# A decoder step on one core: convolution projected by block with its products on VectorE, embedding projections moved ahead of their gate

## The reference, cut to what matters

```python
xn = rmsnorm(h, g_mix)
z = xn @ w_in
q, k, v, og, lr, cv = jnp.split(z, SPLITS, axis=-1)
...                                   # gated linear attention gives o
a, gate = jnp.split(cv, 2, axis=-1)
u = a * jax.nn.sigmoid(gate)
c, buf_new = causal_depthwise_conv(u, buf0, w_conv, b_conv)   # 31 taps, 512 channels
c = jax.nn.silu(layernorm(c, g_conv_ln, b_conv_ln))
h = h + jnp.concatenate([o, c], axis=-1) @ w_out
xn = rmsnorm(h, g_ffn)
h = h + hier_moe(xn, ...)             # 32 experts, 2 for each row
xn = rmsnorm(h, g_ple)
h = h + jax.nn.sigmoid(xn @ w_ple_gate) * (p_l @ w_ple_proj)
...
return rmsnorm(h, g_final)
```

## Time and profile before

| | before |
|---|---|
| median of 3 runs | 1126.66 us (1126.3 to 1128.25) |
| the profiled execution's own time | 1125.14 us |
| its span in the trace | 1123.3 us |
| busy share of the span | TensorE 90%, VectorE 64%, ScalarE 42%, GpSimd 26% |

### The profile page before, as it was taken

How to read it: one execution, slowest core, us unless ns; L and a number is a source line. 1 busy time by engine, 2 the same in 40 slices (tenths; PEclk the granted TensorE clock), 3 DMA queues, 4 the chain that set the end, 5 groups by cost and what they waited for, 6 DMA issues and landing times.

```text
span 1123.3 us, 14888 instructions
## 1 busy us (share of the span) xinstructions
PE 1008.9 (90%) x4992; PEld 546.8 (49%) x4992; DVE 721.1 (64%) x830; ACT 473.6 (42%) x721; POOL 295.3 (26%) x267
## 2 busy tenths in 40 slices
PE   4899979999999978999429999999999999399996
PEld 3555535555555545555314555544444454144442
DVE  6259866667667596443586777776667675556552
ACT  7333122323222542322315655566555454434553
POOL 0567234656511522111011222222222223000000
PEclk9999989999999969999659999999999999699998
DMA  7443040000000602222647999999999977523321
GB/s 256 123 133 124 3 19 1 1 0 0 0 0 1 213 36 75 75 83 90 268 179 277 391 380 366 342 368 361 361 365 361 355 290 259 222 89 102 108 69 60
DMA packets 52234, 191.13 MB, mean 170 GB/s; under 512 B 19601, under 2 KB 20898, under 8 KB 37218
## 3 DMA queue, kind: packets, MB, share of 16 engines
q1 hardware_dynamic: 41250, 172.76, 43.6%
q0 software_dynamic: 10944, 17.85, 4.4%
HBM read 181.50 MB, written 31.09 MB: 189 GB/s over the span
## 4 chain that ended last, share of the span: by engine, by line
PE 63%; DVE 15%; DMA 11%; issue 4%; ACT 4%; POOL 2%; DVEq 1%; SPq 0%; POOLq 0%; ACTq 0%
PE psum L1691 12%; PE psum L1920 11%; PE psum L1999 8%; PE psum L1834 8%; DVE arena L1238 6%; DMA arena<-xn,ids 6%; PE psum L1938 6%; PE psum L1907 3%; PE psum L1989 2%; PE psum L1876 1%; PE psum L1758 1%; PE psum L1757 1%; DVE arena L1511 1%; DMA arena<-in_w_ple 1%; PE psum L1761 1%
## 5 line engine op out<-in xcount | busy, mean ns | idle before, releaser
L1920 PE MATMUL psum<-arena 128*128 128x512 f16 x888 | 201.8, 385 | 4.4 <-DVE arena L1515 4.4
L1238 DVE SCALAR_TENSOR_TENSOR arena<-arena,wc x120 | 185.9, 1549 | 17.3 <-DVE arena L1238 17.0
L1511 DVE TENSOR_TENSOR arena<-arena 128x1024 f16<-128x1024 f32 x148 | 174.2, 1217 | 2.6 <-ACT arena L1077 2.6
L1691 PE MATMUL psum<-arena 128*128 128x512 f16 (+1 forms) x864 | 153.1, 331 | 0.6 <-ACT arena L914 0.6
L1077 ACT ACTIVATE arena<-arena 128x1024 f16<-128x1024 f32 x148 | 147.1, 1047 | 0.0
L1920 PEld LDWEIGHTS psum<-arena 128*128 128x128 f16 x888 | 87.6, 99 | 104.6 <-DVE arena L1515 5.0
L1938 PE MATMUL psum<-arena 128*128 128x512 f32 x296 | 133.2, 593 | 1.2 <-DVE arena L1549 1.2
L1691 PEld LDWEIGHTS psum<-arena 128*128 (+1 forms) x864 | 68.2, 98 | 78.2 <-issue 8.7
L1683 PE MATMUL psum<-arena 128*128 128x384 f16 x576 | 96.3, 331 | 4.4 <-DVE arena L1205 2.4
L1999 PE MATMUL psum<-arena 128*128 128x512 f16 x432 | 96.8, 385 | 2.5 <-DVE arena L1620 2.5
L800 POOL DMA_INDIRECT yrows<-arena,idy x31 | 35.0, 1130 | 239.6 <-DVE arena L1549 232.0
(11 more groups left out here) (239 smaller groups left out, 1267.2 us busy)
## 6 DMA issues: line engine op xcount, KB each, us to landing
arena<-in_w_gu SPq DMA_DIRECT2D x74, 1024.0 KB, 9.3
arena<-in_w_dn SPq DMA_DIRECT2D x37, 1024.0 KB, 7.2
arena<-yrows SPq DMA_DIRECT2D x18, 512.0 KB, 4.7
side<-in_w_tok SPq DMA_DIRECT2D x16, 388.0 KB, 3.3
arena<-in_x SPq DMA_DIRECT2D x9, 512.0 KB, 4.4
side<-in_x SPq DMA_DIRECT2D x9, 512.0 KB, 4.0
xn<-arena SPq DMA_DIRECT2D x9, 512.0 KB, 2.9
out_y<-arena SPq DMA_DIRECT2D x9, 512.0 KB, 3.0
```

The lines of the kernel that those rows point to most:

```text
L1238: dve.scalar_tensor_tensor(acc, src, w[:, k:k + 1], acc, ALU.mult, ALU.add).then_inc(conv, 1)
L1511: dve.tensor_tensor(wsp[s][1][:, part], wgu[s][:, part], wsp[s][0][:, part], ALU.subtract).then_inc(ws_lo, 1)
L1691: x = pe.matmul(out, xnT[w][:, k, bass.ds(n * P, P)], wtok[m][:, k, col:col + width], start=k + w + m == 0, stop=k == KC - 1 and w == 1)
L1920: x = pe.matmul(psum[:, 2 + s, :], xgT[s][w][:, k, :], wsp[s][m][:, k, :], start=k + w + m == 0, stop=k == KC - 1 and w == 1)
```

## The change

In the conv stage TensorE's groups are taken by block: gate and a of one block of 384 rows, then the next block, in banks 2b and 2b+1. The first block is put between the transposes of tiles 3 to 8. ScalarE evacuates only the gate (the sigmoid); VectorE multiplies a straight from PSUM by it (`glu_rows`), and VectorE takes over both low parts of the splits. GpSimd keeps only the split of the first chunk, both halves of it. 18 taps of each of chunks 0 and 1 stand in this stage (`REST` is 13 instead of 9), four between one block and the next, so 88 taps (11 a step) are left for the attention stage. The transfers of the first chunk's weights and of the identity matrix come earlier.

For the embedding, `w_proj` and all nine tiles of `pT` are loaded in the router stage into buffers that the attention left. All nine projections run on TensorE between the experts and the gate; ScalarE copies each from PSUM to SBUF (`proj_out`), in turns with the split of `w_ple`, and `finish` reads that copy.

```diff
+        prj = [at(w, D) for w in [R4, R4 + D, RT + 2048, *[R1 + D * k for k in range(2, 6)], R4 + 7992, R4 + 7992 + D]]
...
+        wproj = [[th[:], qk[:]], [PT[:].rearrange("p a b -> p (a b)"), v_sb[0][:]]]
...
+            for k in range(PC):
+                for half in range(2):
+                    sp.dma_start(wproj[k][half], a["w_proj"][:, k, half * 512:(half + 1) * 512]).then_inc(pT_in, 16)
+            for n in range(NT):
+                sp.dma_start(pT[n], a["pT"][n]).then_inc(pT_in, 16)
             load_gu(2, 0, 2)
...
             def load_ple():
-                sp.dma_start(wproj, a["w_proj"]).then_inc(pw_in, 16)
...
+            pl.wait_ge(wcv_in, 16)
+            pl.tensor_copy(wcv[0][0], wcv_raw).then_inc(wcv_hi, 1)
+            pl.wait_ge(wcv_hi, 1)
+            pl.tensor_tensor(wcv[0][1], wcv_raw, wcv[0][0], ALU.subtract).then_inc(wcv_lo, 1)
...
+                for b in range(NBLK):
+                    if c >= 1:
+                        act.wait_ge(u_rdy, 4 * (c - 1) + GLU[b])
+                    act.wait_ge(cv_ps, 6 * c + 2 * b + 1)
+                    act.activation(sg_sb[:, b * BLK:(b + 1) * BLK], psum[:, 2 * b, 0:BLK], ACT.Sigmoid).then_inc(cv_sb, 1)
+                    for k, half in pieces_beside(c, b):
+                        split_wt(k, half)
...
+            def proj_out(n):
+                act.wait_ge(pr_ps, n + 1)
+                if n >= 3:
+                    act.wait_ge(wl_lo, KC + n)
+                act.activation(prj[n].rearrange("p (a b) -> p a b", b=512), psum[:, 4 - 2 * (n % 2):6 - 2 * (n % 2), :],
+                               ACT.Copy).then_inc(pr_sb, 1)
...
-            REST = 9
+            REST = 13
...
+            def block_done(c, b):
+
+                if b == 0 and c + 1 < CC:
+                    split_cv(c + 1)
+                glu_rows(c, b)
+                for k, half in pieces_beside(c, b):
+                    split_wt(k, half)
+
+            for b in range(NBLK):
+                block_done(0, b)
+            STEP = 4
+            for i in range(2 * (K - REST)):
+                taps(i // (K - REST), i % (K - REST), 1, i)
+                if i % STEP == STEP - 1:
+                    n = NBLK + i // STEP
+                    block_done(n // NBLK, n % NBLK)
...
-                dve.tensor_tensor(mixd[j], mixd[j], psum[:, 4:6, :].rearrange("p a b -> p (a b)"), ALU.mult).then_inc(mix_rdy, 1)
+                dve.wait_ge(pr_sb, n + 1)
+                dve.tensor_tensor(mixd[j], mixd[j], prj[n], ALU.mult).then_inc(mix_rdy, 1)
...
             def embed(n, j):
                 gate_half(n, j, 0)
-                if late(n, 1):
-                    project_p(n, j)
                 if not (isinstance(n, int) and n == NT - 1):
                     turn_x3(n + 1, 1 - j)
                 gate_half(n, j, 1)
...
+            pe.wait_ge(u_rdy, 4 * CC)
             pe.wait_ge(wt_lo, 2 * KC)
...
+            pe.wait_ge(pT_in, 16 * (2 * PC + NT))
+            for n in range(NT):
+                project_p(n)
+                if n == 6:
+                    turn_x3(0, 0)
             pe.wait_ge(wl_lo, 2 * KC)
+            pe.wait_ge(pr_sb, NT - 1)
             embeds(pe, embed)
```

More of the change, by code:

```diff
@@ L302, in bass_decoder_step @@
         og = [at(RT + 2304, VW), v_sb[1][:]]
+        wproj = [[th[:], qk[:]], [PT[:].rearrange("p a b -> p (a b)"), v_sb[0][:]]]
+        pT = [*[side[1][:, PC * j:PC * (j + 1), :] for j in range(KC // PC)],
+              *[v_sb[1][:, PLE * j:PLE * (j + 1)].rearrange("p (a b) -> p a b", b=P) for j in range(VW // PLE)],
+              *[x[:].rearrange("p (a b) -> p a b", b=P) for x in (E2, la, absx)]]
         wr = sb("wr", KC, G + NE)
@@ L444, in bass_decoder_step @@
         pw_in = sem("pw_in")
-        pT_in = [sem(f"pT_in{j}") for j in range(2)]
+        pT_in = sem("pT_in")
+        pr_sb = sem("pr_sb")
         add_rdy = sem("add_rdy")
-        std3_rdy = sem("std3_rdy")
-        rst3_rdy = sem("rst3_rdy")
         xn3_rdy = sem("xn3_rdy")
@@ L470, in rows, with pieces_beside @@
             return t[bass.ds(n * P, P), :]
[L472 to L483, removed]
+        def pieces_beside(c, b):
+            k = NBLK * c + b
+            return [(k, half) for half in range(2)] if k < KC else []
         block = ctx.enter_context(nc.Block())
@@ L511, in _ @@
             sp.dma_start(brb[:], a["b_router"].to_broadcast([P, G + NE])).then_inc(c_in, 16)
+            for k in range(1, KC):
+                if k % NBLK == 0:
+                    load_cv(k // NBLK + 1)
+                for half in range(2):
+                    load_wt(k, half)
             for cc in range(CC):
                 sp.dma_start(us[:, cc, :, 0:HIST], a["state_conv"][:, cc]).then_inc(hist_in, 16)
[L514 to L518, removed]
             sp.wait_ge(zero, 1)
@@ L684, in _ @@
             pl.memset(St[:], 0.0).then_inc(zero, 1)
[L685 to L706, removed]
+            pl.wait_ge(wcv_in, 16)
+            pl.tensor_copy(wcv[0][0], wcv_raw).then_inc(wcv_hi, 1)
+            pl.wait_ge(wcv_hi, 1)
+            pl.tensor_tensor(wcv[0][1], wcv_raw, wcv[0][0], ALU.subtract).then_inc(wcv_lo, 1)
+            pl.wait_ge(wcv_lo, 1)
+            pl.wait_ge(u_rdy, 4 * CC)
             pl.memset(oraw[NS:P, NT - 1, :], 0.0).then_inc(zero, 1)
@@ L907, in _ @@
                     split_cv(c + 1)
[L908 to L913, removed]
-                        act.activation(dst[:, b * BLK:(b + 1) * BLK], psum[:, 3 * part + b, 0:BLK], fn).then_inc(cv_sb, 1)
+                for b in range(NBLK):
[5 more added lines that the diff above has]
+                        split_wt(k, half)
             def lr_out(n):
@@ L1177, in _, with split_gate @@
             act.wait_ge(wple_in, 16 * KC)
-            for k in range(KC):
+            def split_gate(k):
                 if k == 1:
@@ L1190, in _ @@
         def _(dve):
-            dve.wait_ge(g1_in, 32)
+            dve.wait_ge(g1_in, 16)
             def norm_x(n, j):
@@ L1669, in transpose_x, with conv_part @@
                 x.then_inc(xT_ps, 1)
-            tiles(pe, transpose_x)
+            def conv_part(c, b, part, chunks):
+                col = P - P * part
+                for k in chunks:
+                    for w, m in PASSES:
+                        x = pe.matmul(psum[:, 2 * b + part, 0:BLK], wcv[c % 2][w][:, k, col:col + P],
+                                      xnT[m][:, k, b * BLK:(b + 1) * BLK], start=k + w + m == 0,
+                                      stop=k == KC - 1 and w == 1)
+                return x
@@ new lines, in _ @@
+            for n in range(4):
+                transpose_x(n, n % 2)
+            pe.wait_ge(wcv_lo, 1)
+            pe.wait_ge(xnT_v, 3)
+            for part in range(2):
+                for q in range(2):
+                    x = conv_part(0, 0, part, range(4 * q, 4 * q + 4))
+                    if q:
+                        x.then_inc(cv_ps, 1)
+                    n = 4 + 2 * part + q
+                    transpose_x(n, n % 2)
+            pe.wait_ge(xnT_v, 6)
+            for part in range(2):
+                for q in range(2):
+                    x = conv_part(0, 1, part, range(4 * q, 4 * q + 4))
+                    if q:
+                        x.then_inc(cv_ps, 1)
+                    elif part == 0:
+                        transpose_x(NT - 1, 0)
```

125 lines of the change are left out of this document (72 added, 53 removed).

## The result

The changed kernel took 1107.03 us (median of 4 runs, 1106.55 to 1108.17), the kernel before on the same chip 1126.49 us. The ratio is 0.9825, with a 95% interval of 0.9808 to 0.9842: faster by 19.5 us, where 13 were forecast. The span of the profiled execution fell from 1123.3 to 1104.9 us, so 18.4 us are to be accounted for.

What follows compares the result with a forecast made beforehand. Bounds: VectorE's late, slow list ending the conv stage, and a VectorE-ScalarE circle in the embedding. Terms -12.8 + 0.7 + 0 - 1.0 = -13.1 take 1125.14 to 1112.0; plus 1.5 to the median, about 1113.5 us, range 1105 to 1122.

Steps and rivals of the forecast that it cites:

- term 1: Conv stage into the attention: the first `turn` comes 12.8 us earlier, between 9 and 17.
- 36 taps at 1.28 + 0.18: Conv stage, VectorE's list: taps of 1.28 us with gaps of 0.18 take 52.7 us.
- TensorE waits some 7 us for VectorE: End of the conv stage: TensorE's blocks end near 123, VectorE's last product at 130.2.
- the 1.7 us for waking: Start of the attention: TensorE, waking from idle, loses 1.4 to 2 us before the first `turn`.
- term 2: Attention stage: eleven taps a step instead of ten are covered by reserves, costing 0.7 us in all.
- term 3: Router stage: 1.9 MB more loads cost 0 us, or 5 us without the DMA engines' idle time as cover.
- term 4: Embedding, with projections moved ahead of the gate: 1.0 us less, between 3 less and 2 more.
- the circle: Embedding loop: VectorE and ScalarE hand each tile to and fro, 14.45 to 14.8 us a tile.
- (a): Embedding loop: TensorE alone bounds it, -22.5 us in place of -1.0, about 1092 us; 6%.
- (b): Conv stage: slow taps or late transfers put the last product at 140; gain only 3, about 1123 us; 7%.
- (c): Embedding loop: TensorE's clock falls; mildly, 2 us a tile, mostly hidden; throughout, about 1183 us; 4%.
- (d): Router stage's loads not covered, or experts' gathers fall worse: 5 us more, 1118.5 us; 10%.

Runs made afterwards that it cites:

- experiment 5: The changed kernel with the 16 low parts of the attention weights back on GpSimd; 1102.89 us, ratio 0.9785.
- experiment 7: The changed kernel with 28 taps in the conv stage instead of 36 and 12 in each attention step; 1110.7 us, ratio 0.9863.
- experiment 6: The changed kernel with all transposes first and then the conv blocks in order; 1114.71 us, ratio 0.9892.
- experiment 3: The kernel before with the conv stage's taps written out instead of a hardware loop; 1120.47 us, ratio 0.9954.
- experiment 8: The changed kernel with the gate's sigmoid ahead of a later tile's square and the root's table loaded right after it; 1093.08 us, ratio 0.9697.
- Experiment 4: The changed kernel with the embedding gate's sigmoid replaced by a plain copy, so without its table loads; 1087.71 us, ratio 0.9652.

## Why the prediction was right, and where its terms were off

**The bound at the end of the conv stage (term 1)** was predicted at -12.8 us and measured at -19.6. The mechanism held: TensorE's wait for VectorE's taps went, block 0 moved between the transposes, GpSimd's absence made taps short. The step that failed is "36 taps at 1.28 + 0.18", and with it "TensorE waits some 7 us for VectorE". The 0.18 belongs to the hardware loop, and the changed list is written out: seven groups of four took 5.24 each, and the two with a chunk's shorter first tap 4.8 and 4.6, 46.1 in place of 52.7. The first tap came 2.2 us later than forecast (59.89), the last product 5.0 earlier (125.18 against 130.2), and by then VectorE was waiting for TensorE. Experiments 5 and 7 show it from both sides: slower taps or fewer of them leave the first `turn` at 144.1 to 144.2, and experiment 6 shows that what delays TensorE's list moves it one for one. Since TensorE hardly idles, the 1.7 us for waking did not fall due either. The two make 4.7 at the start of the projections (125.60 against 130.3) and 2.1 behind it. I had the count of instructions between two taps in front of me, in the listing of VectorE's order, and priced the new list by the old one's gap.

The cast on GpSimd, taken at 4 us between bounds of 2 and 4.06, took 2.73, and the subtraction 4.06 again. The rest of it went elsewhere, in the timeline of the change:

```profile
12.02 2.73 POOL L683 CAST arena<-arena 128x2048 f16<-128x2048 f32 x1 [9.97 <-DMA arena<-in_w_cv]
...
14.84 4.06 POOL L685 TENSOR_TENSOR arena<-arena 128x2048 f16<-128x2048 f32 x1
...
15.17 4.82 DVE L1199 SCALAR_TENSOR_TENSOR arena<-arena,rst,g 128x1024 f32<-128x1024 f32 x1 [0.15 <-DVE rst L1195]
...
24.00 4.00 PE L1713 MATMUL psum<-arena 128*128 128x384 f16 x12 [0.79 <-DVE arena L1205]
```

VectorE's scaling of a tile stood beside the subtraction and took 4.82 us where others took 1.28. Block 0 started at 24.00, not 21.

**Eleven taps a step (term 2)**: +0.7 predicted, +1.5 measured at the last `scores`. The steps themselves took it without a wait, as forecast; the last tap was mis-sized. I had set VectorE's slack of 0.81 us against it. But it stands ahead of qkT too, where no slack was left: TensorE's wait there grew from 2.23 to 3.71, by one whole tap. Another 1.5 us between the first and the last `turn` are the fourth long step (1.58 us), and 2.2 more came by the first `gate_up`. There too a lower clock is part of it: eight transposes at 425.70 took 1.97 us after the change and 1.09 at the same place before. The prediction had no term for this. The experts then gave 1.1 us back. That is within what this stage varies by with the same instructions: from the first `gate_up` to the first projection it took 367.3 us in experiment 3, 372.1 before, 371.0 after and 373.8 in experiment 8.

**Router stage (term 3)**: 0 predicted and measured. From the last of the router's matmuls to the experts' first transposes it is 34.67 us against 34.54. The DMA engines did the added 1.9 MB and stood still before `load_gu(2)` was issued at 562.78, as said. The columns are those of the earlier trace rows:

```profile
552.00:558.00 6.00, 0.54 (x9) 0.41 (x9) 5.69 (x13) 0.00 (x0) 0.00 (x0) 0.50 0.74 243
558.00:564.00 6.00, 0.54 (x9) 0.41 (x9) 5.26 (x12) 0.00 (x0) 2.57 (x2) 0.50 0.13 14
```

**Embedding (term 4)**: -1.0 predicted, -3.0 measured, within its bounds. The timeline of the change:

```profile
941.78 1.02 PE L2050 MATMUL psum<-th,side 128*128 128x512 f32 x2
...
973.55 5.34 PE L2060 MATMUL psum<-arena 128*128 128x512 f16 x24
...
980.87 1.22 DVE L1657 TENSOR_TENSOR arena<-psum,arena 128x1024 f16<-128x1024 f32 x1 [6.05 <-ACT arena L1129]
...
1010.91 5.35 PE L2060 MATMUL psum<-arena 128*128 128x512 f16 x24 [2.51 <-DVE arena L1657]
...
1025.57 7.04 PE L2060 MATMUL psum<-arena 128*128 128x512 f16 x24 [2.67 <-DVE arena L1657]
...
1093.99 1.02 ACT L1135 ACTIVATE arena<-psum 128x1024 f32<-128x1024 f32 x1 [3.42 <-PE psum L2060]
```

The nine projections ran through, and the gate started 31.8 us behind the first of them (32.4 forecast). Tile 1's `x3T_out` came 5.1 us later against the first projection than before (5.8). Then seven tiles to 1082.15 took 101.3 us, 14.47 each, where I had written 102.6 for "14.45 to 14.8" (1.3 of the difference), and from there it was 11.84 to the sigmoid (11.8). Experiment 4 shows that the circle set this.

**The rivals.** (a) fell: it needs the circle out of the way, and with its table loads gone the kernel took 1087.7 us, TensorE alone setting the time of the first tiles only. (b) fell, the last product being at 125.18. (c) held in its mild form: at two tiles (1025.57 and 1069.04) the granted clock fell after a wait and 24 matmuls took 7.04 us instead of 5.35. Both were covered by the circle and cost nothing at the end. The Trainium skill, TensorE: Matmul & The Clock Gate, "HAM oscillation — how this bites in real kernels", describes a fall at every step of a loop that waits some 3 to 5 us for a DMA each time. Here the waits are 1.3 to 2.7 us, and a fall came at two of eight tiles; waits of 2.51 and 2.59 us passed without one. (d) fell with term 3. 

So the 5.3 us between the forecast and the measured shift of the span are: term 1 6.8 too small, term 4 2.0, the experts 1.1, less 0.8 of term 2 and 3.8 of the clock and the output projection. The forecast time was off by 1.1 us more, since it added 1.5 us to come from one execution to the median, and the changed kernel's profiled execution (1107.1) is its median.

## What to carry to other kernels

Price a moved instruction by its own duration, and look up separately what stands between it and its neighbour: a gap that comes from a hardware loop doesn't move with the work. Then set the new lists of the two engines side by side and ask which one ends last before giving a wait to either; here one wrong gap was enough to turn the bound around. And when a stage is a circle over several engines, work taken out of a non-binding engine gains little until the circle itself is shortened, but it can be what makes shortening it possible: the same edit of ScalarE's order gave 12 us with the projections' bank out of the ring and cost 15 with it in, both by the traces.

## What the runs showed of the hardware

- VectorE's taps (two SBUF inputs, 1024 wide) took 1.28 to 1.31 us alone. Beside GpSimd's subtraction of 128x776 they averaged 2.02 us in experiment 5 (16 taps, 32.3 us), while a product with one input in PSUM stayed at 0.54. GpSimd itself was slowed too, from 1.66 to 2.46 us on the mean for a piece (12 pieces, 29.5 us).
- A hardware loop on VectorE put 0.18 us between taps that depend on each other; written out, four that depend on each other took 5.24 us together, with no gap in the trace. Which part of the loop's work makes the gap was not tried.
- ScalarE's change between the tables of sigmoid and root cost 1.28 us each time, and the next instruction followed at once (1009.15 to 1010.45). It cost the kernel only where it stood inside the circle: experiment 8 has as many loads in a tile as the change.
- The granted clock of TensorE fell in some attention steps and not in others with the same instructions and no idle time, each long step costing 1.58 us. One step of experiment 3 took 28.00 us at a clock of 0.88.
